# Feed-forward in three chunks (6, 8 and 8 inner tiles), with the down products of the last two as 2x2 block products in 7 multiplications

## What is computed

```
x = x + 0.5 * (silu(rms(x) @ w_gate1) * (rms(x) @ w_up1)) @ w_down1
h = rms(x);  p = h @ w_in               # then mLSTM and retention heads
x = x + concat(y_mlstm, y_retention) @ w_out
x = x + 0.5 * (silu(rms(x) @ w_gate2) * (rms(x) @ w_up2)) @ w_down2
y = rms(x)
```

## Time and profile before

| | us |
|---|---|
| median of 3 runs | 1064.79 (1064.61 to 1065.61) |
| span of the profiled execution | 1063.2 |
| TensorE matmuls busy | 1055.5, 8425 matmuls recorded |
| VectorE busy | 684.2 |
| ScalarE busy | 465.7 |
| GpSimd busy | 189.8 |

### The profile page before, as it was taken

The page is one execution under the profiler, slowest core; times in us unless marked ns, Lnnn a source line. Parts: engine busy times, 40 slices in busy tenths (PEclk is TensorE's granted clock), DMA queues, the critical chain, the costliest instruction groups (busy, mean ns, idle before and its releaser), DMA issues.

```text
span 1063.2 us, 20510 instructions
## 1 busy us (share of the span) xinstructions
PE 1055.5 (99%) x8425; PEld 1052.1 (99%) x8425; DVE 684.2 (64%) x1170; ACT 465.7 (44%) x822; POOL 189.8 (18%) x169
## 2 busy tenths in 40 slices
PE   9999999999999999999999999999999999999997
PEld 8999999999999999999999999999999999999997
DVE  6997752367866676655655556598875236777555
ACT  6466641256652345433222224446664114666323
POOL 1122100112201211210332222212210002220111
PEclk9999999999999999999999999999999999999999
DMA  8589482479833377445454224547958328892422
GB/s 225 121 172 200 100 196 84 96 159 177 176 82 96 64 135 139 71 68 80 69 80 75 67 78 62 140 91 170 206 110 187 92 82 166 178 180 52 124 75 84
DMA packets 245493, 127.84 MB, mean 120 GB/s; under 512 B 9228, under 2 KB 243892, under 8 KB 245272
## 3 DMA queue, kind: packets, MB, share of 16 engines
q1 hardware_dynamic: 207032, 106.79, 41.6%
q0 software_dynamic: 38288, 19.72, 14.6%
q10 hardware_dynamic: 80, 0.02, 0.0%
HBM read 123.22 MB, written 3.29 MB: 119 GB/s over the span
## 4 chain that ended last, share of the span: by engine, by line
PE 98%; DMA 1%; DVE 0%; SPq 0%; issue 0%; ACT 0%
PE dense L623 52%; PE dense L768 31%; PE core_banks L768 5%; PE core_banks L623 3%; PE dense L691 1%; PE core_banks L928 1%; PE core_banks L943 1%; PE dense L824 1%; PE core_banks L946 1%; PE core_banks L918 1%; DMA x_tok<-in_x_prompt 1%; PE core_banks L955 0%; PE core_banks L912 0%; PE core_banks L914 0%; PE core_banks L805 0%; PE core_banks L666 0%
## 5 line engine op out<-in xcount | busy, mean ns | idle before, releaser
L1481 DVE TENSOR_TENSOR w_lo<-w_raw,w_hi 128x1024 fp32r<-128x1024 f32 (+2 forms) x118 | 131.7, 1133 | 55.1 <-ACT w_hi L1068 55.0
L1068 ACT ACTIVATE w_hi<-w_raw 128x1024 fp32r<-128x1024 f32 (+2 forms) x118 | 105.2, 904 | 89.3 <-PE dense L623 81.4
L623 PE MATMUL dense<-h_hi,w_hi 128*128 128x272 f32 x684 | 142.5, 290 | 0.0
L623 PE MATMUL dense<-xg_hi,w_hi 128*128 128x272 f32 x672 | 142.2, 293 | 0.0
L623 PE MATMUL dense<-h_lo,w_hi 128*128 128x272 f32 x684 | 141.1, 287 | 0.0
L623 PE MATMUL dense<-h_hi,w_lo 128*128 128x272 f32 x684 | 140.9, 287 | 0.0
L623 PE MATMUL dense<-xg_lo,w_hi 128*128 128x272 f32 x672 | 138.9, 288 | 0.0
L623 PE MATMUL dense<-xg_hi,w_lo 128*128 128x272 f32 x672 | 138.8, 287 | 0.0
L768 PE MATMUL dense<-x_op_hi,w_lo 128*128 128x272 f32 x432 | 124.6, 289 | 0.0
L768 PE MATMUL dense<-x_op_hi,w_hi 128*128 128x272 f32 x432 | 124.5, 288 | 0.0
L768 PE MATMUL dense<-x_late_hi,w_lo 128*128 128x272 f32 x432 | 124.5, 288 | 0.0
(11 more groups left out here) (341 smaller groups left out, 2212.1 us busy)
## 6 DMA issues: line engine op xcount, KB each, us to landing
w_raw<-in_w_ffn_up SPq DMA_DIRECT2D x91, 256.0 KB, 3.6
w_src<-in_w_ffn_gate SPq DMA_DIRECT2D x90, 256.0 KB, 4.6
w_raw<-in_w_in SPq DMA_DIRECT2D x32, 512.0 KB, 8.9
w_raw<-in_w_ffn_down SPq DMA_DIRECT2D x32, 384.0 KB, 4.0
w_raw<-in_w_ffn_down SPq DMA_DIRECT2D x32, 320.0 KB, 3.5
w_src<-in_w_ffn_gate POOLq DMA_DIRECT2D x36, 256.0 KB, 5.2
w_raw<-in_w_ffn_up POOLq DMA_DIRECT2D x36, 256.0 KB, 5.8
w_raw<-in_w_out SPq DMA_DIRECT2D x8, 512.0 KB, 3.9
```

What stands on the lines that cost most here:

```text
L623: last = nc.tensor.matmul(out[:, half, 0:TH], w[:, s % 4, k, :], x(kt)[:, half * TH:(half + 1) * TH], start=start and n == 0 and m == 0, s ...
L1068: nc.scalar.activation(w_hi[:, s % 4, 0:k_tiles(s), :], raw, ACT.Copy).then_inc(w_hi_ready, 1)
L1481: nc.vector.tensor_tensor(w_lo[:, s % 4, 0:nk, :], w_raw[:, s % RAW, 0:nk, :], w_hi[:, s % 4, 0:nk, :].bitcast(F32), ALU.subtract).then_in ...
```

## The change

- Three chunks: the first of 6 inner tiles (the 4 plain ones and one pair), then 8 and 8. `PAIRS` becomes (2, 8, 8) steps. The down product of the first chunk stays plain (288 matmuls per feed-forward); those of the other two are 4 steps each of 7 products (`down_pair`): two output tiles, two halves of the columns, the chunk's even and odd tiles as halves of k.
- For that the inner values h of each pair are needed as the 7 operands of the block form: VectorE makes four sums of 272 columns (`sum_h`), and 7 operands of 272 columns are split (`h_to_hi`, `h_to_lo`) where 2 tiles of 544 were.
- The weights of the down steps go through the same loads, accumulating DMAs, sums and splits as those of the pairs.
- Every product of a down step is added to x from PSUM by itself (`take_down`: 7 instructions of 272 columns).
- `kept` is gone: ScalarE copies products 0, 1 and 2 straight into the gate or h buffer, the 4th copy (product 4) is dropped, and VectorE adds to the copy in place. Product 6 waits for `gate_second` or `up_second` where it waited for that copy.
- No arithmetic on GpSimd in the feed-forwards: the squares at the end of each are made by ScalarE and added by 5 accumulating DMAs; VectorE adds the last ones.
- The end: both last output tiles come out of the last down step; the output is stored in the order 0, 1, 2, 3, sample.

The chunks and two orders of products:

```diff
-    PAIRS = (range(0, 8), range(8, 18))
-    FC, F0 = (12, FT - 12), (0, 12)
+    PAIRS = (range(0, 2), range(2, 10), range(10, 18))
+    FC, F0 = (STD + 2, 8, 8), (0, STD + 2, STD + 10)
+    FIRST_ORDER = (0, 1, 3, 2, 4, 5, 6)
+    LAST_ORDER = (0, 1, 3, 2, 5, 4, 6)
```

TensorE in a pair's step and in a down step (`OPENS` is products 0, 1 and 3; `down_pair`'s first part is for d = 0):

```diff
             def pair(n, c, p):
...
                     if o == 6:
-                        pe.wait_ge(product_copied, 4 * P_ + 4)
+                        if e == 0:
+                            pe.wait_ge(pair_gate_made, 3 * Q + 2)
+                        else:
+                            pe.wait_ge(pair_up_taken, 3 * Q + 2)
...
+            def down_pair(n, c, d):
...
+                    k = (c - 1) * GROUPS + last_k
+                    pe.wait_ge(h_op_lo_ready, lo_made(n, k - 1, H_LO[-1]))
+                    for o in OPENS:
+                        pe.wait_ge(block_lo, BLOCKS * g + o + 1)
+                        part(o, range(last_k))
+                    for o in OPENS:
+                        pe.wait_ge(h_op_lo_ready, lo_made(n, k, o))
+                        part(o, range(last_k, KH)).then_inc(product_done, 1)
+                    pe.wait_ge(down_taken, BLOCKS * D + 1)
...
+                    part(2, range(KH)).then_inc(product_done, 1)
...
+                    part(5, range(KH // 2))
+                    pe.wait_ge(down_taken, BLOCKS * D + 4)
...
+                    part(4, range(KH)).then_inc(product_done, 1)
...
+                    part(5, range(KH // 2, KH)).then_inc(product_done, 1)
+                    pe.wait_ge(down_taken, BLOCKS * D + 5)
...
+                    part(6, range(KH)).then_inc(product_done, 1)
+                    return
+                turns = {}
+                if n and c == 2:
+                    turns = {2: 2 * d - 2, 4: 2 * d - 1} if d == DOWNS - 1 else {3: 2 * d - 2, 5: 2 * d - 1}
+                for rank, o in enumerate(order_of(g)):
+                    if rank in turns:
+                        turn_out(turns[rank])
+                    before = {2: 0, 4: 2, 5: 1, 6: 4}
+                    if o in before:
+                        pe.wait_ge(down_taken, BLOCKS * D + order_of(g).index(before[o]) + 1)
...
+                    part(o, range(KH)).then_inc(product_done, 1)
```

ScalarE in a down step:

```diff
+            def down_pair(n, c, d):
...
+                for o in range(BLOCKS):
+                    next_hi(n, g, o)
+                    if c == 2 and d and o in (1, 4):
+                        j = 2 * d - 2 + (o == 4)
+                        x_ready(n, j)
+                        if n == 0:
+                            normed_hi(0, j, None, G_MIX, 0)
+                        else:
+                            times_gain(j)
+                        square_end(n, j)
```

VectorE:

```diff
             def gate_second(n, p):
-                dve.wait_ge(product_copied, 4 * pair_index(n, p) + 4)
-                nc.vector.tensor_tensor(pair_gate[1][:, TH:T], kept[:, 0, 3, :], kept[:, 0, 1, :], ALU.add).then_inc(pair_gate_made, 1)
+                dve.wait_ge(product_done, done_by(step_of_pair(n, p), 4))
+                dve.wait_ge(product_copied, 3 * pair_index(n, p) + 2)
+                out = pair_gate[1][:, TH:T]
+                nc.vector.tensor_tensor(out, pair_banks(0)[0], out, ALU.subtract).then_inc(pair_gate_made, 1)
...
+            def take_down(n, c, d, o):
+                dve.wait_ge(product_done, done_by(g, o))
...
+                x = xT[:, 2 * d + m, half * TH:(half + 1) * TH]
+                nc.vector.scalar_tensor_tensor(x, pair_banks(g % 2)[BANK[o]], factor, x, ALU.mult, ALU.add).then_inc(down_taken, 1)
...
+                    if deferred:
+                        for h_o in ((), (1,), (2,), (4, 5), (), (), ())[o] if e == 0 else ():
+                            sum_h(n, k, h_o)
+                        for h_o in (((), (), (), (), (0,), (1,), (3,)), ((2,), (4,), (5,), (6,), (), (), ()))[e][o]:
+                            h_to_lo(n, k, h_o)
```

More of the change, by code:

```diff
@@ L74, in hybrid_trunk_step @@
     U_STD = (U_F1, U_F2)
-    U_DOWN = [[u + 2 * STD + 2 * DT * c for c in range(2)] for u in U_STD]
+    U_DOWN = [u + 2 * STD for u in U_STD]
     X_ORDER = (0, 1, NC, 2, 3)
@@ L85, in hybrid_trunk_step @@
     X_BY_DVE = [piece for piece in X_PIECES if piece != X_BY_ACT]
[L88 to L93, removed]
+    HALF_COLS = [slice(0, TH), slice(TH, T)]
+    END_CHUNKS = [(0, 1), (2, 3, NC)]
+    END_COLS = [slice(0, 2 * P), slice(2 * P, T)]
     DVE_COLS, ACT_COLS = slice(0, 5 * P), slice(5 * P, D)
+    Y_PARTS = (2, 2, 2, 2, 1)
     RAW = 4
@@ L832, in column_sums @@
-            def column_sums(out, source, chunks):
-                for c in chunks:
-                    n = P if c < NC else TS
-                    last = nc.tensor.matmul(out[0:n, c:c + 1], source[:, CH[c]], ones[:, 0:1], start=True, stop=True)
-                return last
-            def turn_last(step):
-                pe.wait_ge(out_taken, DT - 1 if step == 2 else DT - 2)
-                pe.wait_ge(x_gained, DT + step)
-                j = DT - 1
-                for c in END_CHUNKS[step]:
-                    last = nc.tensor.transpose(last_turn(c), x_gain[:, j % 2, CH[c]], ident[:, :])
+                    nc.tensor.transpose(X[:, 2 + j % 2, CH[c]], x_gain[:, j % 2, CH[c]], ident[:, :])
@@ L859, in turn_dummies @@
+                for c in END_CHUNKS[step]:
+                    last = nc.tensor.matmul(final_sum(c), sq_last[:, 0, CH[c]], ones[:, 0:1], start=True, stop=True)
+                last.then_inc(final_sums, 1)
             def turn_dummies(n):
@@ L1520, in sum_t2 @@
-            def sum_t2(n, p):
-                e, P_ = p % 2, pair_index(n, p)
-                dve.wait_ge(block_summed[e][1], 16 * (P_ // 2 + 1))
-                dve.wait_ge(block_loaded[e][5], 16 * (P_ // 2 + 1))
-                if P_ > 1:
-                    dve.wait_ge(block_lo, BLOCKS * (P_ - 1))
+                first_pair(n)
+                pair(n, 0, 1)
+                up_last(n, 1, NP // 2 * n)
+                first_to_lo(n, STD + 1)
+                first_to_lo(n, STD)
+                down(n)
@@ new lines, in ffn, with sum_t2 @@
+                block_to_lo(n, STEPS * n + STEP_DOWN + 1, BLOCKS - 1)
+                for c in (1, 2):
+                    for p in PAIRS[c]:
+                        pair(n, c, p)
+                    for d in range(DOWNS):
+                        down_pair(n, c, d)
+            def sum_t2(g):
+                e = g % 2
+                dve.wait_ge(block_summed[e][1], 16 * (g // 2 + 1))
+                dve.wait_ge(block_loaded[e][5], 16 * (g // 2 + 1))
+                if g > 1:
+                    dve.wait_ge(block_lo, BLOCKS * (g - 1))
```

1122 lines of the change are left out of this document (648 added, 474 removed).

## The result

The changed kernel takes **1128.58 us** (median of 4 runs, 1127.92 to 1129.64) beside 1064.74 us: ratio 1.0596, 95% interval 1.0581 to 1.0611. The forecast was 1101.1 (1080 to 1114): the sign was right, the time lies 27.5 us above it and 14.6 above the end of the range. The profiled execution spans 1126.8 us, 63.6 more than before.

A forecast was written before the change was run, and what follows sets the result against it. TensorE's row of matmuls was taken to bound the kernel. Terms -24.1 + 35.8 + 6.1 + 9.2 + 3.7 + 1.5 + 4.1 = +36.3 on a span of 1063.2 gave 1099.5, with 1.6 for the median 1101.1 us (1080 to 1114).

The forecast's parts named there:

- Matmuls, -24.1: Down products: 960 matmuls per feed-forward instead of 1056, at 0.1253 us each, saving 24.1 us over both.
- Product 6, +35.8: Pair steps: TensorE pauses 0.60, 0.95 or 1.52 us before product 6, waiting for gate_second or up_second; +35.8 us (24 to 46).
- First pair, 2 x 3.04: First pair of each feed-forward: product 6 pauses 3.04 us for a late gate_second; +6.1 us (4 to 8).
- The clock falls: Rival: TensorE at 1.2 GHz for the step behind each 3 us pause, 10.5 us more each; 1122 us, chance 6%.
- the forecast's own signs of being wrong: Pair steps staying at 10.5 us, waits that name DMA, or a clock that drops would show the forecast wrong.
- First down steps, 9.2: First down step of each chunk: pauses of 1.65 and 0.64 us for VectorE's takings; +9.2 us (4 to 14).
- Turning back, 3.7: Last chunk's turning of x: waits on x_gain, 1.68 us, and 0.19 behind product 2, twice; +3.7 us (0 to 5).
- End of the first feed-forward: Before the norm's sums: x's 7th tile comes with product 6, TensorE waits for its square's addition; +1.5 us (0 to 3).
- Costs nothing: ScalarE's 121 more instructions and the loads cost nothing; GpSimd's dropped additions give VectorE time back, off the path.
- Tail, +4.1: Program's end: 1.8 us pause and 2.9 more behind product 6, less 0.6 for transposes; +4.1 us (1 to 6).
- Covered: Rival: gate_second and up_second reach PSUM before product 6 is due, so waits are covered; 1054.6 us, chance 6%.
- half the pauses: Rival: VectorE catches up where TensorE paused before; gate pairs pause 0.6, first downs little; +10, 1074.8 us, chance 8%.

The follow-up runs named there:

- Experiment 3: Changed kernel, but in every pair step except each feed-forward's first VectorE takes gate_second or up_second before splitting block 4: 1101.6 us.
- Experiment 6: Changed kernel, but in each chunk's first down step VectorE takes products 2 and 4 earlier, ahead of sums and splits: 1124.6 us.
- experiment 9: All reorderings combined, VectorE adding all squares (1062.3 us), plus root before second mixer weights' split, a down-step split and a square addition moved later: 1057.7 us.
- experiment 2: Changed kernel, but SyncE holds the loads of the mixer's first weights until the five squares have landed: 1121.7 us.
- Experiments 1: Changed kernel, but VectorE instead of accumulating DMAs adds the five squares at the first feed-forward's end: 1113.3 us.
- experiment 5: Changed kernel with VectorE adding the first feed-forward's squares (1113.3 us), and the mixer's first weights split behind the last two tiles of x: 1112.5 us.
- experiment 4: Changed kernel, but in each feed-forward's first pair VectorE takes gate_first and gate_second ahead of the splits of blocks 0 and 1: 1121.9 us.

## Why the prediction was right or wrong

The sum of +36.3 is 27.3 short of the 63.6 by which the span grew: 21.2 of that lie at the first feed-forward's end, 2.1 and 2.3 in the stretches of the two feed-forwards, 0.9 in the mixer (the slow matmuls behind the sums), 0.7 at the very end and 0.1 at the start.

- **Matmuls, -24.1: right.** Between the first pair's first matmul and the last large one stood 2567 spacings before, 322.0 us or 0.1254 each; now there are 2471, 309.9 us of 337.6. The other 27.6 are pauses and slow matmuls, forecast 25.5; the second feed-forward is like the first.
- **Product 6, +35.8: right to 2%.** Per feed-forward 2 x 0.62, 8 x 0.98 and 6 x 1.53 = 18.2 by the starts, forecast 17.9. The spacings of the trace were the right ones. By the Trainium skill, VectorE: DVE Perf Modes, The DRAIN you can't avoid, taken strictly, the term would be 46, and the trace does not agree with that reading. Experiment 3 took 29.4 of it out by order alone.
- **First pair, 2 x 3.04: right on the pause (2.95), short by the clock.** The slow matmuls cost 1.6 and 1.5 more. "The clock falls" was priced as a whole step at half speed, 10.5, with a chance of 6%; it happened, for 3 to 4 us, and a clock that drops was one of the forecast's own signs of being wrong. That it fell behind both pauses was in part luck. (The Trainium skill, TensorE: Matmul & The Clock Gate, Part 1: idle halves the clock. The traces agree behind 10 of 14 such pauses.)
- **First down steps, 9.2: right.** 1.55 and 0.51 by the starts, with 0.2 of slow starts behind them: 2.3 each, four times. Experiment 6 got back a little more than half by order; most of the rest turned up as four waits one step later, which went in experiment 9, again by order.
- **Turning back, 3.7: nearly.** 1.58 twice; the 0.19 behind product 2 did not show.
- **End of the first feed-forward, "+1.5 (0 to 3)": the step that failed.** It measured 22.7. I followed the last tile (taking, high part, square, addition) and priced the DMAs that add the squares at nothing, and so did "Costs nothing" with the loads, of which I named only the quarter blocks of the steps. Two things were missing. The additions are a chain over one buffer, each square behind the landing of the last addition; the edit shows that, and the nearest row, GpSimd's accumulating DMAs of weights, gives 5.2 us to landing before and after (below). And the plain down units no longer free the weight slots: the mixer's first loads were issued 17 us ahead of the last large matmul before (365.78 to 383.0), and now wait for the last down step, 8.5 us ahead of it (390.29 to 398.8), beside the additions. Neither makes the loss by itself: with the loads held (experiment 2) the last square had landed 1.2 us behind the last large matmul; together, two landings took 26 us. How much such loads stretch an accumulating DMA stood in no row of before. Experiments 1, 2, 5 and 9 share the loss out. On the way from the last large matmul to the next feed-forward's first pair the change lost 23.5 (369.7 for 346.2): 15.4 of it goes with the DMAs of the squares, 3.5 with the orders of experiments 5 and 9 (350.8 there), and 4.6 stay.

```profile
w_src<-in_w_ffn_gate POOLq DMA_DIRECT2D x36, 256.0 KB, 5.2
```

- **Tail, +4.1: about 5.9.** The pause was 2.0 for 1.8 and the end 3.6 for 2.9, and some 0.9 of slow matmuls lie behind the pause, where the clock fell to 0.50; less the 0.6 for transposes, which was not looked at by itself.
- **Rivals.** "Covered" and "half the pauses" did not happen. The case that happened was not among them: a resource of the next stage reached backwards into this one.
- Open: how much of the last 4.6 at the first feed-forward's end is the late loads. In experiment 9 the norm's sums come 1.9 later than before (forecast 1.5, the work of the last tiles); the other 2.8 lie in the mixer, where TensorE pauses 2.4 and then loses 1.6 to the clock. An earlier issue of those loads was not tried.

## What to carry to other kernels

Price a pause from the row of work behind its last common release, by spacings of starts and not by durations; that held to 0.03 us for the pauses before product 6. But where a stage ends, list what every queue issues for the *next* stage, when it is released before and after, and what shares its path: here more than half of the miss was one buffer filled again only after a DMA that had company, and behind it stood a load that had been issued 17 us ahead of the stage's last matmul and now was 8.5 us ahead. An order that frees one wait is worth only what the next one behind it leaves: experiment 5 moved the sums by 5 us and the next pair by 0.1. And where the clock may fall behind a pause, lay two profiles side by side stretch by stretch before believing a difference of 1 or 2 us in their spans.

## What the runs showed of the hardware

- A DMA of 272 KB that adds one SBUF tile to another lands in 3.3 to 3.6 us without the next stage's loads, in 15.5 and 10.5 beside them (512 KB each in rows of 512 bytes, then a table and states).
- TensorE's clock: behind pauses of 0.5 to 1.6 us the granted clock still reads 1.00 and one or two matmuls start 0.1 late. Behind 2.95 us it fell to 0.50 in 10 of 14 places, for 3 to 6 us. Behind about 2 us it went either way: it fell behind the 2.0 before the last turning in the changed kernel, 1.4 us after TensorE had begun again, and stayed at 1.00 behind the 1.9 of experiment 4.
- A VectorE instruction of 128x544 took 1.96 us in the kernel before beside GpSimd's additions (1.36 us each), and 0.77 without them (L1486 and L2128).
